# A state-space layer's entry and its scan: rows stored unscaled by column halves, scan cut into quarters

## The chip, the core and the metric

The kernel runs on one core of a Trainium2 chip. The metric is the device time of the whole program in microseconds (us). Engines are named as the profile names them: PE (matrix products; PEld are its weight loads), DVE (vector), ACT (activations and copies), POOL, and SP, whose queue (SPq) issues most DMAs. Each engine works through its own instructions in order; semaphores connect them.

## The reference, cut to what matters

The program is a two-layer encoder over 512 tokens of 1024 columns. The change touches the seam between the layers: the gated per-layer embedding that ends layer 0, the root-mean-square norm that opens layer 1, and the state-space mixer (S5) behind it.

```
h  = h + sigmoid(rmsnorm(h, norm_ple[0]) @ ple_gate[0]) * (p[0] @ ple_proj[0])
hn = rmsnorm(h, norm_mix[1])          # h * rsqrt(mean(h*h) + eps) * w
u  = hn.reshape(512 tokens, 64 groups, 16 columns)
# per group, 64 complex states, both directions of time:
#   state[t] = lam * state[t-1] + B u[t]      y[t] = Re(C state[t])
y  = s5(u) + backward s5(u) + d_skip * hn
out, gate = split(gelu(y) @ glu_w)    # glu_w: 1024 x 2048
h  = h + out * sigmoid(gate)
```

## The kernel before

A ring of six 1 MB tiles (`ring`, tile `n` in slot `n % 6`) holds every streamed matrix. SP loads tile `n` once tile `n - 6` is released (the list `release`); its queue is one ordered list, and other transfers stand at fixed places of it. ACT rounds each weight tile to a high part and DVE subtracts to get a low part (`split_tile`), after which PE multiplies (`split_product`, L1300). Product 1 is the embedding gate (two column halves of 512, groups `pg00` and `pg01`), product 2 the matrix `glu_w`.

**Entry.** ACT takes the sigmoid of each finished gate bank (L2131). When both halves of a token block `c` (128 tokens, four blocks) are there, DVE multiplies and adds (`embed_add`, L2819 and L2821, 1024 columns at a time). Then ACT squares, DVE scales rows by the norm factor and the weight (`norm(3)`, L2327), and SP moves the result (`s5_moves`): four stores to DRAM (L829), eight loads back (L834) with eight consecutive tokens per partition (`UN`, 64 chunks in each of two column halves, so 16 partitions per load), and the table of decays (L836). ACT waits for all nine loads, reorders by group into `UP` (L2141), PE transposes (L1601, 64 small ones), DVE copies to `U` (L2833).

**Chunk inputs.** PE forms, for each of 16 banks `b` of four groups, the contribution of each eight-token chunk to the states (`chunk_inputs`, L1615, products with only 64 moving columns). ACT drains each bank into `Z` (L2151).

**Scan.** `scan(dve, chain, hf)` runs on DVE for one half of the groups after the other (32 groups): seven steps of four instructions along the chunks of a block (128x512 each), six small ones across the eight blocks (128x64), seven more of four that spread the block starts (128x512). ACT copies each finished slice to `H` (`place_states`, two instructions of 64x512, L819 and L820); the backward direction is mirrored there.

**Outputs.** PE waits for all eight slices of a half (semaphore `s_zb`), then runs `outputs(q)` for four of the eight blocks `q` of eight groups (L1631 and L1634: per group one product with `U` and two with states, 24 per block), each in two banks; ACT applies gelu to each bank (L2161), PE transposes (`turn_outputs`, L1643), ACT and DVE write high and low parts (`gelu_high` L2167, L2840) for product 2. PE starts product 2 when all eight blocks are through.

Of the kernel before, what the change touches and what calls it, by code (L numbers as in the profile page):

```python
# [53 lines left out]
def build_program(nc, I, out):  # L54
# [27 lines left out]
    with ctx:  # L82
# [245 lines left out]
        s_hnd = sem("hn_in_dram")  # L328
        s_un = sem("s5_inputs_by_chunk")
        s_upA = sem("s5_inputs_by_group")  # L330
# [87 lines left out]
        def unit_after_block(i):  # L418
# [3 lines left out]
            if i == 3:  # L422
# [55 lines left out]

        f_high, f_low = [[sbuf_r[:, a:a + TILE].rearrange("p (k n) -> p k n", k=4)
                          for a in (ffa_end.at + m * TILE, ffa_end.at + (m + 1) * TILE)] for m in (0, 2)]  # L480
# [199 lines left out]
        HALF = G5 // 2  # L680
# [52 lines left out]
        def decays(ap):  # L733
# [3 lines left out]
        s5a = Arena(sbuf, base, words)  # L737
        U = s5a.take(G5 * NC5).rearrange("p (g n) -> p g n", g=G5)
        un_at = s5a.at
        UN = s5a.take(L5 * D // 2).rearrange("p (t n) -> p t n", t=L5)  # L740
        ZW = 2 * NC5 * HALF
        z_at = [s5a.at, s5a.at + ZW]
        h_at = [s5a.at + 2 * ZW, s5a.at]
        s5a.take(3 * ZW)
        Z, H = [[sbuf[:, a:a + ZW].rearrange("p (e s j g) -> p e s j g", e=2, s=8, j=8) for a in at] for at in (z_at, h_at)]
        lamR, lamI = decays(s5a.take(3 * L5 * G5))
        UP = sbuf[:, z_at[1]:z_at[1] + L5 * D // 2].rearrange("p (q g t c) -> p q g t c", q=4, g=8, t=L5)
        una = Arena(sbuf, un_at, un_at + L5 * D // 2)
        s_at = [una.at, una.at + 2 * 8 * HALF]
        S5 = [una.take(2 * 8 * HALF).rearrange("p (e s g) -> p e s g", e=2, s=8) for _ in range(2)]  # L750
        scan_tmp = [una.take(16 * HALF).rearrange("p (e s g) -> p e s g", e=2, s=8) for _ in range(2)]
        Yb = [una.take(L5 * P).rearrange("p (t n) -> p t n", t=L5) for _ in range(2)]
        gtmp = sbuf[:, base + 5 * D:base + 5 * D + 2048].rearrange(v4, a=4)
        hn_dram = nc.dram_tensor("hn_by_token", (T, D), F32, kind="Internal").ap()
# [4 lines left out]
            3: lambda e, c: e.wait_ge(s_ph, c + 1),  # L759
            4: lambda e, c: e.wait_ge(s_drD, cumD[gidx["go1"]] - 3 + c),  # L760
            5: lambda e, c: e.wait_ge(s_mc, c + 1),
            6: lambda e, c: e.wait_ge(s_ph, 4 + c + 1),
# [14 lines left out]
        def scan(dve, chain, hf):  # L777

            z, st, (a, b) = Z[hf], S5[hf], scan_tmp
            wide = [P, 2, 8, HALF]  # L780
            of_half = slice(HALF * hf, HALF * (hf + 1))
            real = lambda j: lamR[:, j - 1, of_half].unsqueeze(1).unsqueeze(1).broadcast_to(wide)
            imag = lambda j: lamI[:, j - 1, :, of_half].unsqueeze(2).broadcast_to(wide)

            def product_sum(old, swapped, j, add, new):
                chain.link(dve.tensor_tensor(new[0], old, real(j) if len(old.shape) == 4 else real(j)[:, :, 0, :], ALU.mult))
                chain.link(dve.tensor_tensor(new[1], swapped, imag(j) if len(old.shape) == 4 else imag(j)[:, :, 0, :], ALU.mult))
                dve.wait_ge(chain.sem, chain.n - 1)
                chain.link(dve.tensor_tensor(new[0], new[0], add, ALU.add))
                chain.settle()  # L790

            for j in range(1, 8):
                swapped = bass.AP(sbuf, z_at[hf] + ZW // 2 + (j - 1) * HALF, [[words, P], [-ZW // 2, 2], [8 * HALF, 8], [1, HALF]])
                product_sum(z[:, :, :, j - 1, :], swapped, 1, z[:, :, :, j, :], (a, b))
                chain.link(dve.tensor_tensor(z[:, :, :, j, :], a, b, ALU.add))
                chain.settle()
            chain.link(dve.memset(st[:, :, 0, :], 0.0))
            chain.link(dve.tensor_copy(st[:, :, 1, :], z[:, :, 0, 7, :]))
            chain.settle()
            for n in range(2, 8):  # L800
# [354 lines left out]
        def _(pe):  # L1155
# [490 lines left out]
            for q in range(8):  # L1646
                chunk_inputs(q)
# [1475 lines left out]
```

## Time and profile before

| | us |
|---|---|
| median of 3 runs (2834.9 to 2839.12) | 2835.84 |
| the profiled execution, as timed | 2841.83 |
| its span, first to last instruction | 2839.9 |
| its mean granted TensorE clock (1.00 is 2.4 GHz) | 0.938 |

PE is busy 89% of the span, DVE 60%, ACT 44%. All times of the trace count from the start of the span. The stretch of the change runs from 1122 us, where the gate product is under way, to 1334.7 us, where product 2 starts; everything behind depends on it. In the page's line of PE's busy tenths this stretch holds the lowest digits of the span's second half (4, 7, 6).

### The profile page before, as it was taken

The numbers are of one execution on the slowest core, as the hardware profiler recorded it, in microseconds if no ns is written. First come the engines' busy times: TensorE is split into PE (matmuls) and PEld (weight loads), VectorE is DVE, ScalarE is ACT, GpSimd is POOL, SyncE is SP. The second block draws the span as 40 slices with busy tenths as digits, with TensorE's granted clock in tenths as the row PEclk, the third lists the DMA queues.
The fourth block names the chain that finished last, engine by engine and source line by source line (L and its number), as shares of the span: only waits on it lengthen the run. The fifth ranks groups of instructions, "written<-read, shape, count | busy, mean of one in ns | idle before, by whom it ended". The sixth has DMA issues, their size and how long they took to land.

```text
span 2839.9 us, 31193 instructions
## 1 busy us (share of the span) xinstructions
PE 2539.9 (89%) x12509; PEld 2037.2 (72%) x12509; DVE 1700.9 (60%) x1870; ACT 1249.7 (44%) x1359; POOL 239.2 (8%) x240
## 2 busy tenths in 40 slices
PE   4889898889999998476949999999999999999977
PEld 2445464468887876476849988898889988898853
DVE  5697788332323223284256678766876778677852
ACT  2343333032222213353225567555765567566741
POOL 3012845000000000000000000000000000000010
PEclk9999989999999999558969999999999999999989
DMA  8446510122322231524046779877997689767950
GB/s 232 139 140 184 149 60 30 52 72 91 104 89 89 91 117 60 130 104 186 30 163 228 241 281 371 285 252 245 358 333 252 240 311 366 270 238 251 381 202 30
DMA packets 317023, 528.70 MB, mean 186 GB/s; under 512 B 19302, under 2 KB 175562, under 8 KB 314218
## 3 DMA queue, kind: packets, MB, share of 16 engines
q1 hardware_dynamic: 287690, 481.83, 49.6%
q0 software_dynamic: 6000, 26.27, 2.9%
q10 hardware_dynamic: 23184, 18.55, 2.0%
q8 instruction: 101, 1.65, 0.2%
q14 instruction: 48, 0.39, 0.0%
HBM read 497.05 MB, written 47.91 MB: 192 GB/s over the span
## 4 chain that ended last, share of the span: by engine, by line
PE 79%; DVE 9%; ACT 3%; issue 3%; POOL 3%; DMA 2%; SPq 0%; ACTq 0%; DVEq 0%; POOLq 0%
PE psum L1698 25%; PE psum L1300 16%; PE psum L1757 11%; PE psum L1558 5%; PE psum L1759 4%; PE psum L1198 4%; PE psum L1221 3%; PE psum L1615 2%; DVE stages_r L2994 1%; PE psum L1634 1%; ACT stages_r L2213 1%; PE psum L1369 1%; POOL stages L1023 1%; POOL stages L1026 1%; PE psum L1175 1%
## 5 line engine op out<-in xcount | busy, mean ns | idle before, releaser
L2994 DVE TENSOR_TENSOR stages_r<-kept,stages_r 128x2048 fp32r<-128x2048 f32 x336 | 769.1, 2291 | 274.0 <-ACT stages_r L2213 273.2
L1698 PE MATMUL psum<-stages_r 128*128 128x512 f32 x3136 | 751.7, 398 | 21.0 <-DVE stages_r L3049 11.1
L2213 ACT ACTIVATE stages_r<-kept 128x2048 fp32r<-128x2048 f32 x336 | 637.3, 1912 | 266.1 <-PE psum L1698 140.4
L1698 PEld LDWEIGHTS psum<-stages_r 128*128 128x128 f32 x3136 | 593.2, 191 | 149.5 <-DVE stages_r L2994 12.4
L1757 PE MATMUL psum<-stages_r 128*128 128x320 f32 x1792 | 464.8, 345 | 6.3 <-issue 3.2
L1300 PE MATMUL psum<-stages_r 128*128 128x512 f32 x1920 | 442.8, 393 | 17.2 <-DVE stages_r L2773 17.2
L1300 PEld LDWEIGHTS psum<-stages_r 128*128 128x128 f32 x1920 | 365.1, 190 | 94.2 <-issue 17.7
L1759 PE MATMUL psum<-stages_r 128*128 128x160 f32 x1792 | 423.1, 236 | 0.0
L1759 PEld LDWEIGHTS psum<-stages_r 128*128 128x128 f32 x1792 | 342.8, 191 | 2.0
L1757 PEld LDWEIGHTS psum<-stages_r 128*128 128x128 f32 x1792 | 337.0, 188 | 9.0 <-DVE stages_r L2994 3.8
L2773 DVE TENSOR_TENSOR stages_r<-kept,stages_r 128x2048 fp32r<-128x2048 f32 x54 | 123.5, 2292 | 363.1 <-ACT stages_r L2093 363.1
L2093 ACT ACTIVATE stages_r<-kept 128x2048 fp32r<-128x2048 f32 x54 | 103.1, 1915 | 349.8 <-PE psum L1300 245.9
L1558 PE MATMUL psum<-stages_r,stages_front_r 128*128 128x512 f32 x672 | 154.5, 392 | 6.8 <-DVE stages_front_r L2792 6.8
L1558 PEld LDWEIGHTS psum<-stages_r,stages_front_r 128*128 128x128 f32 x672 | 127.4, 190 | 33.8 <-issue 7.2
L1221 PE MATMUL psum<-stages,kept 128*128 128x512 f32 x256 | 118.5, 608 | 0.8 <-ACT stages L1860 0.8
L1198 PE MATMUL psum<-kept,stages 128*128 128x512 f32 x256 | 112.2, 600 | 1.6 <-ACT stages L1860 0.8
L2249 ACT ACTIVATE stages<-stages 128x160 f32<-128x160 f32 x112 | 37.8, 338 | 158.2 <-DVE stages L3026 158.2
L1198 PEld LDWEIGHTS psum<-kept,stages 128*128 128x128 f32 x256 | 49.1, 193 | 62.8 <-issue 60.8
L1105 POOL DMA_INDIRECT stages<-moe_rows_by_token,stages x8 | 18.3, 2290 | 891.6 <-PE psum L1706 521.4
L1221 PEld LDWEIGHTS psum<-stages,kept 128*128 128x128 f32 x256 | 47.2, 193 | 54.4 <-issue 53.3
L3029 DVE TENSOR_TENSOR kept<-stages 128x160 f32<-128x160 f32 x112 | 36.6, 327 | 45.2 <-ACT stages L2249 45.2
L1175 PE MATMUL psum<-kept,stages 128*128 128x128 f32 x160 | 26.7, 341 | 39.5 <-DVE stages L2327 39.2
(379 smaller groups left out, 2512.4 us busy)
## 6 DMA issues: line engine op xcount, KB each, us to landing
kept<-in_moe_w_gu_dram SPq DMA_DIRECT2D x224, 1024.0 KB, 6.5
kept<-in_moe_w_down_dram SPq DMA_DIRECT2D x112, 1024.0 KB, 6.4
kept<-in_ffn_w_gu_dram SPq DMA_DIRECT2D x28, 1024.0 KB, 5.1
kept<-in_ev_w_in_dram SPq DMA_DIRECT2D x16, 1024.0 KB, 6.4
kept<-in_ffn_w_down_dram SPq DMA_DIRECT2D x14, 1024.0 KB, 5.1
s_output_maps_by_state<-stages ACTq DMA_DIRECT2D x64, 128.0 KB, 2.0
s_input_maps<-stages ACTq DMA_DIRECT2D x32, 256.0 KB, 2.5
s_output_maps<-s_output_maps_by_state SPq DMA_DIRECT2D x32, 256.0 KB, 4.9
```

Source lines behind the costliest of these rows:

```text
L1198: m = pe.matmul(psum[:, b0 + b, 0:width], act[:, 4 * kk + k, b * P:(b + 1) * P], w[:, k, 0:width], **at)
L1221: m = pe.matmul(psum[:, b, :], *pair, start=kk == 0 and k == 0, stop=kk == 1 and k == 3)
L1300: m = pe.matmul(psum[:, 4 * (g % 2) + b, :], *pair, start=kk == 0 and k == 0 and n == 0, stop=kk == 1 and k == 3 and n == 2, skip_group_ch ...
L1558: m = pe.matmul(psum[:, 2 * c + hf, :], a[:, k, at], w[hf][:, k, :], start=j == 0 and k == 0 and n == 0, stop=j == FJ - 1 and k == 3 and n ...
L1615: m = pe.matmul(psum[:, b % 8, (2 * gl + e) * NC5:(2 * gl + e + 1) * NC5], w[:, 4 * i + gl, e, :], U[:, 8 * q + 4 * i + gl, :], start=True ...
L1698: m = pe.matmul(out_, a, b, start=start and n == 0, stop=stop and n == len(pairs) - 1, skip_group_check=True)
L1757: pe.matmul(bank[:, 0:2 * CAP], wh[:, k, fs], x_[:, k, :], start=k == 0, stop=False, skip_group_check=True)
L1759: m = pe.matmul(bank[:, 0:CAP], wl[:, k, fs], x_[:, k, 0:CAP], start=False, stop=k == 7, skip_group_check=True)
L2093: act.activation(f_high[t % 2], ring[:, n % RING, :].rearrange("p (k n) -> p k n", k=4), ACT.Copy).then_inc(s_wh, 1)
L2213: act.activation(w_high[n % WSLOTS], unit_tile(n), ACT.Copy).then_inc(s_wh, 1)
L2773: dve.tensor_tensor(f_low[t % 2], ring[:, (SPLIT_RUNS[run][1] + t) % RING, :].rearrange("p (k n) -> p k n", k=4), f_high[t % 2], ALU.subtr ...
L2994: dve.tensor_tensor(w_low[n % WSLOTS], unit_tile(n), w_high[n % WSLOTS], ALU.subtract).then_inc(s_ws, 1)
```

## The change

**Entry by halves.** The embedding is added for columns 0 to 511 as soon as gate group `pg00` is drained, and for the rest after `pg01` (`embed_half`). SP stores the half `h` unscaled and loads it back at once (`s5_rows(sp, j)`: four stores of 128x512, four loads of 16 partitions with 16 KB each); the first half stands in SP's queue ahead of two weight tiles, the second behind them. Sums of squares go by halves on ACT (`entry_squares`), are brought into the order of `UN` by eight small products on PE with a selection matrix `pick`, and give a factor `ers` per token. ACT and DVE apply it while they reorder into `UP` (four slices each); the norm weight comes in when DVE moves the transposes to `U` (`ew`). `norm(3)`, its weight load and the full-width add are gone, and the decays come last. PE transposes the first half of the groups, does two chunk blocks, then transposes the second.

**Scan by quarters.** `Z`, the states and the tables are cut into four quarters `v` of 16 groups. A move (`along`, `across`, `spread`) is four instructions; `advance` issues several independent moves together, so that one fills the other's waits. Spreading is by block `q` of eight groups, in two pieces `r` of four and three slices. `place_states(act, q, r)` follows each piece with 3 or 5 copies on ACT, standing between the gelus of the block before. PE waits for `s_zb >= q + 1` before each `outputs(q)`. The two wide waits before product 2 become waits for four parts each.

On SP's queue, first before. `s_input_maps` are 1 MB tiles for the chunk inputs; `dense_bank_done` ends a gate group.

```order
L897 DMA kept<-s_input_maps 128x2048 [waits dense_bank_done]
L897 DMA kept<-s_input_maps 128x2048 [waits ring_tile_used]
L897 DMA kept<-s_input_maps 128x2048 [waits dense_bank_done]
L829 DMA hn_by_token<-stages 128x1024 [waits hn_ready] x4
L834 DMA stages<-hn_by_token 16x8x512 [waits hn_in_dram]
```

And with the change:

```order
L951 DMA kept<-s_input_maps 128x2048 [waits dense_bank_done]
L878 DMA h_by_token<-kept 128x512 [waits ple_added] x4
L882 DMA stages<-h_by_token 16x4096 [waits h_in_dram] x4
L951 DMA kept<-s_input_maps 128x2048 [waits ring_tile_used]
L951 DMA kept<-s_input_maps 128x2048 [waits dense_bank_done]
L878 DMA h_by_token<-kept 128x512 [waits ple_added] x4
L882 DMA stages<-h_by_token 16x4096 [waits h_in_dram] x4
L887 DMA stages<-s_decays 128x1536 [waits dense_bank_done]
```

One half of the round trip has moved ahead of two tiles; the second stands behind them.

On ACT, before, at the start of the outputs. `s5_states_scanned` counts DVE's slices, `s5_y_done` PE's output banks.

```order
L819 ACTIVATE stages<-stages 64x16x32 [waits s5_states_scanned]
L820 ACTIVATE stages<-stages 64x2x8x32
L2161 ACT_TABLE_LOAD
L2161 ACTIVATE stages<-psum 64x4x8x16 [waits s5_y_done] x4
L2167 ACTIVATE stages_r<-psum 128x8x64 [waits gelu_transposed]
```

And with the change, from the second gelu of a block on:

```order
L2249 ACTIVATE stages<-psum 64x4x8x16 [waits s5_y_done]
L855 ACTIVATE stages<-stages 64x16x3x8 [waits s5_states_scanned]
L859 ACTIVATE stages<-stages 64x8x3x8 x2
L863 ACTIVATE stages<-stages 64x16x8
L864 ACTIVATE stages<-stages 64x2x8x8
L2255 ACTIVATE stages_r<-psum 128x8x64 [waits gelu_transposed]
L2249 ACTIVATE stages<-psum 64x4x8x16 [waits gelu_transposed,s5_y_done]
```

The placing of the next block has moved between the gelus; the five copies end what `outputs(q + 1)` waits for.

On DVE with the change, one call of `advance` in the second quarter: an `along` move (256 elements) beside both pieces of a `spread` (512 and 384).

```order
L837 TENSOR_TENSOR stages<-stages 128x256 [waits dve_chain]
L838 TENSOR_TENSOR stages<-stages 128x256
L837 TENSOR_TENSOR stages<-stages 128x512
L838 TENSOR_TENSOR stages<-stages 128x512
L837 TENSOR_TENSOR stages<-stages 128x384
L838 TENSOR_TENSOR stages<-stages 128x384
L842 TENSOR_TENSOR stages<-stages 128x256 [waits dve_chain]
L842 TENSOR_TENSOR stages<-stages 128x512 [waits dve_chain]
L842 TENSOR_TENSOR stages<-stages 128x384 [waits dve_chain]
```

Before, every second instruction of a step waited for the one just ahead of it.

```diff
@@ scan
-            for j in range(1, 8):
-                swapped = bass.AP(sbuf, z_at[hf] + ZW // 2 + (j - 1) * HALF, [[words, P], [-ZW // 2, 2], [8 * HALF, 8], [1, HALF]])
-                product_sum(z[:, :, :, j - 1, :], swapped, 1, z[:, :, :, j, :], (a, b))
-                chain.link(dve.tensor_tensor(z[:, :, :, j, :], a, b, ALU.add))
-                chain.settle()
...
+        SPREAD = ((4, 4), (1, 3))
+        def spread(q, r):
+            v, in_v, (j, n) = q // 2, slice(GB * (q % 2), GB * (q % 2 + 1)), SPREAD[r]
...
+        def advance(dve, chain, finals, done, *moves):
+            for kind, old, swapped, real, imag, add, new, (a, b) in moves:
+                if kind in done:
+                    dve.wait_ge(*done[kind])
+                chain.link(dve.tensor_tensor(a, old, real, ALU.mult))
+                chain.link(dve.tensor_tensor(b, swapped, imag, ALU.mult))
...
+        def place_states(act, q, r):
+            v, g0, (j, n) = q // 2, GB * (q % 2), SPREAD[r]
+            act.wait_ge(s_zf, 2 * q + r + 1)
+            at = slice(g0, g0 + GB)
+            act.activation(H[v].rearrange("p e s j g -> p (e s) j g")[0:NS, :, j:j + n, at], Z16[v][0:NS, :, j:j + n, at], ACT.Copy)
+            for e in range(2):
...
+                m = act.activation(backward, Z[v][NS:P, e, :, j:j + n, at], ACT.Copy)
+            if r:
...
+                act.activation(H[v][0:NS, :, :, 0, at], S5[v][0:NS, :, :, at], ACT.Copy)
+                m = act.activation(backward, S5[v][NS:P, :, :, at], ACT.Copy)
+                m.then_inc(s_zb, 1)
@@ SP
+        def s5_rows(sp, hf):
...
+                sp.dma_start(h_dram[hf, c * P:(c + 1) * P, :], half_h).then_inc(s_hnd, 16)
+            for c in range(TC):
+                sp.wait_ge(s_hnd, 16 * TC * (hf + 1))
...
+                if n == s5_tile0 + RING - 2:
+                    s5_rows(sp, 0)
                 if n == s5_tile0 + RING:
-                    s5_moves(sp)
+                    s5_rows(sp, 1)
+                    s5_decays(sp)
@@ PE
+            turn_inputs(0)
+            chunk_inputs(0)
+            chunk_inputs(1)
+            turn_inputs(1)
+            for q in range(2, 8):
+                chunk_inputs(q)
+            pe.wait_ge(s_vd, 16)
             for q in range(8):
-                chunk_inputs(q)
-            for q in range(8):
-                if q % 4 == 0:
-                    pe.wait_ge(s_vd, 16)
-                    pe.wait_ge(s_zb, 8 * (q // 4 + 1))
                 outputs(q)
-                if q % 4:
+                if q:
                     turn_outputs(q - 1)
...
-            pe.wait_ge(s_glA, 8)
-            pe.wait_ge(s_glD, 8)
+            turn_outputs(7)
             split_product(2)
@@ ACT
+            for t in range(L5 // 2):
+                act.activation(UP[:, :, :, t, :].rearrange("p q g c -> p (q g) c"), UN[:, t, :].rearrange("p (g c) -> p g c", c=GC),
+                               ACT.Copy, scale=ers[:, t:t + 1]).then_inc(s_entA, 1)
...
+            for r in range(2):
+                place_states(act, 0, r)
             for q in range(8):
-                if q % 4 == 0:
-                    place_states(act, q // 4)
-                gelu(2 * q)
-                gelu(2 * q + 1)
...
+                for r in range(2):
+                    gelu(2 * q + r)
+                    if q < 7:
+                        place_states(act, q + 1, r)
+                if q:
                     gelu_high(q - 1)
@@ DVE
+            for j in range(1, 8):
+                move(along(3, j), *([across(2, j)] if j > 1 else []), *(block(2 + j // 3) if j in (2, 5) else []))
+            turn_states(2)
+            first_super(3)
+            for n in range(2, 8):
+                move(across(3, n), *(block(3 + n // 2) if n in (2, 4) else []))
+            gelu_low(0)
+            gelu_low(1)
+            turn_states(3)
+            move(*block(6))
+            move(*block(7))
```

## Rows read from the trace of the kernel before

**Rows 1.** Busy time by windows (start:end, us, busy and count per engine, then PEclk, DMA)
```profile
1142.00:1178.00 36.00, 0.10 (x1) 0.00 (x0) 8.04 (x8) 6.98 (x12) 1.07 (x2) 0.55 0.87 197
1186.00:1200.00 14.00, 13.75 (x65) 13.75 (x65) 0.19 (x1) 6.22 (x6) 0.00 (x0) 0.50 0.20 76
...
1261.00:1265.00 4.00, 4.00 (x20) 4.00 (x21) 3.93 (x7) 1.07 (x1) 0.00 (x0) 0.50 0.00 0
1265.00:1287.00 22.00, 21.96 (x202) 21.32 (x201) 21.06 (x52) 7.28 (x11) 0.00 (x0) 1.00 0.38 145
...
1335.00:1340.00 5.00, 5.00 (x13) 3.84 (x13) 1.77 (x1) 0.00 (x0) 0.00 (x0) 0.50 1.03 382
```
**Rows 2.** The chain that ended last, 1153 to 1424 us (start, us, what)
```profile
1153.64 2.92 DMA hn_by_token<-stages
...
1161.71 15.61 DMA stages<-s_decays
...
1178.55 6.93 PE psum L1601 x64
...
1186.25 54.89 PE psum L1615 x256
...
1243.27 17.60 issue
...
1287.43 15.60 issue
...
1334.71 89.90 PE psum L1300 x384
```
**Rows 3.** The entry in order of time (start, us, engine, line, [idle before <-releaser])
```profile
1122.81 2.29 DVE L2773 TENSOR_TENSOR stages_r<-kept,stages_r 128x2048 fp32r<-128x2048 f32 x1 [9.01 <-ACT stages_r L2093]
...
1142.14 0.60 ACT L2131 ACTIVATE stages<-psum 128x512 f32<-128x512 f32 x1 [2.12 <-PE psum L1300]
...
1177.35 3.90 ACT L2141 ACTIVATE stages<-stages 128x1024 f32<-128x1024 f32 x4 [28.85 <-DMA stages<-s_decays]
```
**Rows 4.** Landing times: the eight loads of line 834, and the weight tiles
```profile
DMA to landing us min/median/max: 5.4/10.1/14.5
...
kept<-s_input_maps SPq DMA_DIRECT2D x8, 1024.0 KB, 4.8
```
**Rows 5.** The scan in order of time on DVE
```profile
1216.06 0.69 DVE L786 TENSOR_TENSOR stages<-stages 128x512 f32<-128x512 f32 x1 [29.86 <-ACT stages L2151]
1216.66 0.68 DVE L787 TENSOR_TENSOR stages<-stages 128x512 f32<-128x512 f32 x1
...
1218.71 0.69 DVE L786 TENSOR_TENSOR stages<-stages 128x512 f32<-128x512 f32 x1
...
1234.88 0.23 DVE L786 TENSOR_TENSOR stages<-stages 128x64 f32<-128x64 f32 x1
...
1235.67 0.22 DVE L786 TENSOR_TENSOR stages<-stages 128x64 f32<-128x64 f32 x1
```
**Rows 6.** ACT in order of time: the last drain, one placing copy, one gelu
```profile
1241.16 2.10 ACT L2151 ACTIVATE stages<-psum 64x512 f32<-64x512 f32 x2 [1.29 <-PE psum L1615]
1243.29 0.63 ACT L819 ACTIVATE stages<-stages 64x512 f32<-64x512 f32 x1
...
1268.48 0.59 ACT L2161 ACTIVATE stages<-psum 64x512 f32<-64x512 f32 x1 [2.08 <-PE psum L1634]
```
**Rows 7.** The page's groups by line: the smallest ACT copy (128x160, 338 ns)
```profile
L2249 ACT ACTIVATE stages<-stages 128x160 f32<-128x160 f32 x112 | 37.8, 338 | 158.2 <-DVE stages L3026 158.2
```
**Rows 8.** PE in order of time: a matmul after a gap; the transposes of one output block
```profile
97.66 1.03 PE L1256 MATMUL psum<-kept,stages 128*128 128x128 f32 x4 [2.82 <-ACT stages L1913]
...
1315.29 0.71 PE L1643 MATMUL psum<-kept,stages 64*128 64x64 f32 x8
```
**Rows 9.** Windows around two gaps of PE (columns as in Rows 1)
```profile
98.00:99.00 1.00, 1.00 (x5) 0.82 (x4) 0.00 (x0) 0.28 (x1) 1.00 (x1) 0.50 1.04 403
...
1082.90:1085.10 2.20, 0.00 (x0) 0.01 (x1) 2.17 (x4) 0.00 (x0) 0.00 (x0) 1.00 0.46 127
```

More of the change, by code:

```diff
@@ L679, in build_program @@
         M5 = L5 + 1
-        HALF = G5 // 2
+        QUARTERS = 4
+        QW = G5 // QUARTERS
+        GB = 8
         STEP = 2
@@ new lines, in build_program @@
+        pick = ent.take(pick_w)
+        pick_n = bass.AP(sbuf, ent.at - pick_w + NC5 - 16, [[words, P], [NC5, 2], [1, 16]])
+        pick_t = ent.take(L5)
+        ew_rows = ent.take(P).rearrange("p (t c) -> p t c", t=L5)
+        ew = ent.take(G5)
+        esc = ent.take(2 * TC * L5).rearrange("p (j c t) -> p j c t", j=2, c=TC)
+        erms, ers = [ent.take(L5) for _ in range(2)]
+        esq_junk = [ffa_end_junk[:, 512 * n:512 * (n + 1)] for n in range(2)]
+        ENT_SQUARE = lambda n: n + 1
@@ new lines, in advance @@
+        def advance(dve, chain, finals, done, *moves):
[4 more added lines that the diff above has]
+                chain.link(dve.tensor_tensor(b, swapped, imag, ALU.mult))
+            n = chain.n - 2 * len(moves)
+            for i, (kind, old, swapped, real, imag, add, new, (a, b)) in enumerate(moves):
+                dve.wait_ge(chain.sem, n + 2 * i + 1)
+                chain.link(dve.tensor_tensor(a, a, add, ALU.add))
+            n += 2 * len(moves)
+            for i, (kind, old, swapped, real, imag, add, new, (a, b)) in enumerate(moves):
+                dve.wait_ge(chain.sem, n + i + 1)
+                last = finals if kind[0] == "spread" else chain
+                last.link(dve.tensor_tensor(new, a, b, ALU.add))
+                done[kind] = (last.sem, last.n)
@@ L2825, in _ @@
             norm(2, parts=True)
-            for t in range(4):
-                split_tile(1, t)
-            embed_add(0)
-            norm(3, False)
+            split_tile(1, 0)
+            split_tile(1, 1)
+            by_chunk = ident.rearrange("p (n t) -> p n t", t=L5)
+            chain.link(dve.memset(pick, 0.0))
+            chain.link(dve.tensor_reduce(out=pick_t, in_=ident.rearrange("p (n t) -> p t n", t=L5), axis=AX_X, op=ALU.add))
+            chain.settle()
+            for i in range(2):
+                chain.link(dve.tensor_reduce(out=pick_n[:, i, :], in_=by_chunk, axis=AX_X, op=ALU.add))
@@ new lines, in move, with block @@
+            def move(*moves):
+                advance(dve, chain, finals, done, *moves)
+            def block(q):
+                return [spread(q, 0), spread(q, 1)]
+            inputs_in(0)
+            for j in range(1, 8):
+                move(along(0, j))
+            first_super(0)
+            for n in range(2, 8):
+                move(across(0, n))
+            turn_states(0)
+            inputs_in(1)
+            for j in range(1, 8):
+                move(along(1, j), *(block(j // 3) if j in (2, 5) else []))
@@ new lines, in _ @@
+            first_super(1)
+            inputs_in(2)
+            for j in range(1, 8):
+                move(along(2, j), *([across(1, j)] if j > 1 else []))
+            turn_states(1)
+            first_super(2)
+            inputs_in(3)
+            for j in range(1, 8):
+                move(along(3, j), *([across(2, j)] if j > 1 else []), *(block(2 + j // 3) if j in (2, 5) else []))
+            turn_states(2)
+            first_super(3)
+            for n in range(2, 8):
+                move(across(3, n), *(block(3 + n // 2) if n in (2, 4) else []))
```

320 lines of the change are left out of this document (198 added, 122 removed).

## The prediction

> **What bounds the kernel now.** I read the chain of waits first, then the windows of busy time, then each engine in order of time. The stretch between the two products is a chain of four parts with nothing beside it. The round trip through DRAM: the last gate sigmoid ends at 1142.7 [rows 3], the last store lands at 1156.6, the decays at 1177.3 behind all the loads [rows 2], and PE has worked 0.10 us of 36 [rows 1]. Transposes and chunk inputs: 1178.55 to 1241.2, PE never free [rows 2]. The scan: after ACT's last drain (1243.3) PE stands 17.6 us, and 15.6 us more between the two halves of the outputs [rows 2]. The outputs and the start of product 2, at 1334.71. What the change is worth is by how much it moves that last time, since product 2 and all behind it keep their length.
>
> **Entry.** DVE finishes its last weight tile at 1125.1 [rows 3] and then adds the first column half: eight instructions of 128x512. Their price I take from the scan. A step of four such instructions takes 2.65 us, one with 64 elements 0.79 [rows 5]; so 1.04 ns per element and 0.52 us of overhead per dependent step of four. Two dependent pairs make 2.9 us, four pairs 5.8, ending at 1130.9. The last store lands 2.9 us later [rows 2], 1133.8. Four loads follow, issued 0.6 us apart. Eight loads landed 5.4 to 14.5 us after their issue [rows 4], so one more every 0.64 + 9.1/7 = 1.94 us. The new loads have the same 256 KB and the same 16 partitions each; I keep the price. First half down at 1133.8 + 5.4 + 3 x 1.94 = 1145.0.
>
> SP has issued two weight tiles behind these loads, the second at about 1142.5. A 1 MB tile alone lands in 4.8 us [rows 4]. The decays landed last of the queue in the old order (15.6 us after issue, where a larger tile takes 4.8), so I take it that one queue is served in order: the tiles, some 2.6 us of transfer each, are through at about 1150, the four second stores (1 MB) about 1153. Without that queueing the stores would land 2.9 us after the add of the last block (1144.2), at 1147.1. Four loads: 1153.1 + 11.2 = 1164.3. ACT and DVE then build `UP` side by side: four ACT copies 3.9 us [rows 3], four on DVE of 1024 elements 4 x 1.14 = 4.6. PE begins at 1168.9 instead of 1178.55: **9.6 us gained**. Its ends: 19 (no queueing, and loads at the rate of tiles) and -7 (loads of 16 KB per partition at half the rate: 2 x 7.8 us more). Sums of squares, `pick`, the eight small products and the factors take no time: they need the last add at 1144.2 and have 20 us of DMA to hide under; without that cover, one square (0.6), a small add, a root and a reciprocal, under 3 us. The four added scalings on DVE are in the 4.6; the weight multiply replaces a copy of equal size. SP's third item, the decays, is wanted only when the scan starts, 17 us on.
>
> Chunk inputs take as long as before, 6.93 + 54.89 us; the second half of the transposes has only changed places. They run at half clock in both [rows 1]. ACT's last drain ends at 1233.7.
>
> **Scan.** `along` on 256 elements: 4 x 0.27 + 0.52 = 1.59 us a step. Beside another move the waits close: 0.60 us from one 512 to the next [rows 5] is 0.53 of elements and 0.07 of overhead, so `along` costs 1.35, `across` (32 elements) 0.41, a block of two spreads 4.3. First quarter: its four banks are drained at 1188.3 (3.5 of transposes, 13.7 of products, 2.1 of drain [rows 6] behind 1168.9); states known at 1204. Second quarter with blocks 0 and 1: from 1205.4 to 1225. Third with the second's `across`: 1238. Fourth with blocks 2 and 3: these end near 1245.5 and 1255; block 4 at 1264.3, block 5 at 1269.7, then two low parts, 6 at 1278.7, 7 at 1283.1.
>
> **Outputs.** After the drain ACT places block 0. A copy costs 0.63 us for 512 elements and 0.338 for 160 [rows 6, 7], so 0.83 ns per element and 0.205 fixed. First piece (512, 256, 256): 1.5; second (384, 192, 192, 128, 128): 1.9. PE starts at 1237.1. It starts at half clock as it did before: 4 us at 1.2 GHz held 20 matmul records, the 22 us behind at 2.4 GHz 202 [rows 1]. At full clock a bank takes 0.59 + 2.08 = 2.67 us from gelu to gelu [rows 6], so a block of two banks and 48 records 5.34, 9 records a us. With 4.1 us at 5 a us first, block 0 takes 7.2, each later one 5.34. Then comes the new wait. The last bank's gelu (0.59 [rows 6]) and the five copies of the second piece (1.9) stand between the end of block q and the start of q + 1: with two handovers of 0.1, 2.7 us, of which PE fills 0.71 with transposes [rows 8]. Behind those copies on ACT only `gelu_high` is queued, which has the next half block to run in. Pace 8.04 us per block. Outputs end at 1237.1 + 7.2 + 7 x 8.04 = 1300.6; the last gelu and eight transposes add 1.5: product 2 may start at 1302.1, **32.6 us earlier**. The entry's 9.6 is in it; so 23 comes from the scan. DVE is ahead of this pace throughout: block 4 is wanted at 1268.5 and is there at 1264.3, the least slack, 4 us.
>
> Product 2 began at half clock, after a gap, and held it for 5.3 us [rows 1, 2]. Now PE comes out of its transposes into it: +2.6 us. Its first tile is fetched when block 5 is out (1284.6) and split on ACT and DVE (2 and 2.3 us) from 1296.4: ready at 1300.7, in time by 1.4 us.
>
> **The clock in the gaps.** PE stands 1.9 us between blocks (2.6 before the second). The clock stayed at 2.4 GHz over an idle 2.2 us and had fallen to 1.2 after one of 2.82 [rows 8, 9]. So I count one fall: 4.1 us at half clock cost 2.0. From both sides: no fall, or one in each of seven gaps, 14.
>
> The Trainium skill ("TensorE: Matmul & The Clock Gate", A second HAM failure mode: psum-queue depth-cycling) says that short pauses between groups of matmuls which cycle through PSUM banks are enough to make the clock swing. By that rule the sum would be that of the first rival below; the row of the 2.2 us gap speaks against it, that of the 2.82 us gap for it.
>
> **The sum.** 32.6 + 2.6 - 2.0 = 33.2. The profiled execution took 2841.83 us (span 2839.9), 6.0 above the median; 2841.8 - 33.2 = 2808.6, and from the median of the runs shown 2835.84 - 33.2 = **2802.6 us**.
>
> **Rivals.**
> 1. *The clock falls in every gap.* For it: the 2.82 us row, and gaps of nearly that size. Against: the 2.2 us row; PE is dense for 5.3 us of 8. Seven falls instead of one: 12 more, 2815.
> 2. *DVE becomes the bound.* The spreads read and write runs of eight elements. ACT's strided drain costs 1.05 us where a copy of the same size costs 0.63 [rows 6], factor 1.67; on the 30 us of spread elements, 20 us more. Block 4 would come 12 us later against 4 of slack, block 7 20 against 9.5: 10 to the end, 2813. The Trainium skill ("Vector Engine (DVE) Microarchitecture Reference", Measured stream behaviour on trn2) says that DVE keeps its full rate as long as elements come in adjacent pairs or longer runs, and loses it only on single hops. By it this rival is void; the drain's single hops and the price of 1.67 agree with it in kind, though they are ACT's.
> 3. *The loads do not keep their rate.* One descriptor per partition instead of eight. At half rate the first loads also delay tiles and stores: 16 worse, 2819. Against: eight loads went by at one steady rate.
> 4. *Slower than before.* The clock stays at half through all outputs, as it stays there for the whole of the chunk inputs though PE is busy 13.75 of 14 us [rows 1]. The place is the gap between blocks; it decides from the point where PE stands there longer than it takes the clock to fall and never climbs. That needs copies of short runs at the drain's price: second piece 3.1 us, placing block 0 5.6, gap 3.9, blocks 10.2 at half clock. 1233.7 + 5.7 + 10.2 + 7 x 14.1 + 2.9 = 1351, 16.5 later than before and the same cold start: 2852. Against: twice the same matmuls lifted the clock after 4 us.
>
> That the change doesn't do what it says isn't open in the order: the halves and quarters stand where the diff puts them. But PE still waits for all 16 drains before the first output, so scan and outputs overlap with each other and not with the chunk inputs; the sum has that.
>
> **How the numbers follow.** The forecast 73%, rival 1 12%, rival 2 6%, rival 3 5%, rival 4 3%, something else 1%. The forecast's own range is 2791 to 2811: 10 down for an entry without queueing and no falls, 8 up for a queue served worse or two or three falls. To leave out no more than 2 in 10 the range reaches over rivals 1 and 2: 2790 to 2818. About 0.2%, 5.7 us, is what a measurement can tell. All cases but rival 4 lie below that: faster 0.95; same 0.02, where two rivals meet; slower 0.03.
>
> **What would show it.** The `UP` slices start near 1164 and the first transposes at 1169; stores of the second half that land 9 us after their add, not 3 (if 3, I am 6 too high). ACT's last drain at 1234. The first output block 7.2 us, later ones 5.3 with 2.7 between starts; a granted clock of 1.00 in nearly all of them. DVE's last spread near 1283, before the last block is wanted. Product 2 at 1302, at full clock. It is wrong if DVE, not ACT's copies, ends the wait of the output blocks, if the clock is 0.50 in them, or if loads take more than 2 us each.

## The result, and the profile after

| | before | after |
|---|---|---|
| median of four runs each, us | 2837.48 (2834.9 to 2839.84) | 2808.14 (2805.14 to 2811.3) |
| ratio, 95% interval | | 0.9897 [0.988, 0.9914] |
| profiled execution: time, span | 2841.83, 2839.9 | 2807.0, 2805.0 |
| mean granted clock of TensorE | 0.938 | 0.944 |
| gate sigmoid (start) to product 2 (start) | 192.6 | 162.2 |
| product 2, us | 89.90 | 87.27 |

The forecast was 2802.6 us; the median is 5.5 above it. The profiled execution is 34.8 us shorter than that of before, where the sum said 33.2.

The chain that ended last, after, over the stretch of [rows 2]:
```profile
1141.60 0.60 ACT stages L2198
...
1143.67 7.49 DMA h_by_token<-kept
...
1152.47 9.08 DMA stages<-h_by_token
1161.64 2.57 ACT stages L2229 x4
1164.45 3.65 PE psum L1671 x32
1168.10 13.84 PE psum L1685 x64
1181.94 3.60 PE psum L1671 x32
1185.54 41.16 PE psum L1685 x192
...
1228.83 3.27 issue
1232.10 0.66 PE psum L1702 x2
```
The chain has the same parts, but the decays no longer end the round trip, the last load of the second half does. PE starts at 1164.45 instead of 1178.55. The two waits of 17.6 and 15.6 us [rows 2] are gone: ACT's placing of the first block holds PE for 3.27, and between the blocks PE now waits seven times, once 2.49 us and six times 1.85, 13.6 in all.

ACT, DVE and SP in order of time at the end of the entry:
```profile
1161.64 2.56 ACT L2229 ACTIVATE stages<-stages 128x512 f32<-128x512 f32 x4 [13.64 <-DMA stages<-h_by_token]
```
```profile
1161.65 1.67 DVE L2956 TENSOR_SCALAR stages<-stages 128x512 f32<-128x512 f32 x4 [13.42 <-DMA stages<-h_by_token]
```
```profile
L882 SPq DMA_DIRECT2D stages<-h_by_token x8: 318/418/420, 1131.9 to 1152.5; - x8
...
DMA to landing us min/median/max: 4.2/7.0/9.3
```
The `UP` slices have 512 elements per partition, not the 1024 of [rows 3], since both halves now lie side by side over 128 partitions.

PE in order of time, four of the eight starts of an output block, and the transposes ahead of one:
```profile
1242.53 0.43 PE L1702 MATMUL psum<-kept,stages 128*64 128x128 f32 x2 [2.49 <-ACT stages L864]
1247.93 0.71 PE L1714 MATMUL psum<-kept,stages 64*128 64x64 f32 x8
1250.49 0.43 PE L1702 MATMUL psum<-kept,stages 128*64 128x128 f32 x2 [1.85 <-ACT stages L864]
...
1260.11 0.43 PE L1702 MATMUL psum<-kept,stages 128*64 128x128 f32 x2 [1.85 <-ACT stages L864]
...
1269.73 0.43 PE L1702 MATMUL psum<-kept,stages 128*64 128x128 f32 x2 [1.85 <-ACT stages L864]
```
Every wait ends with ACT's last placing copy (line 864), none with DVE. ACT in the gap before the second of them:
```profile
1248.04 0.59 ACT L2249 ACTIVATE stages<-psum 64x512 f32<-64x512 f32 x1 [0.66 <-PE psum L1705]
1248.66 0.52 ACT L855 ACTIVATE stages<-stages 64x384 f32<-64x384 f32 x1
1249.19 0.61 ACT L859 ACTIVATE stages<-stages 64x192 f32<-64x192 f32 x2
1249.81 0.31 ACT L863 ACTIVATE stages<-stages 64x128 f32<-64x128 f32 x1
1250.13 0.31 ACT L864 ACTIVATE stages<-stages 64x128 f32<-64x128 f32 x1
```
One gelu and five copies, 2.4 us, priced at 2.5. Windows over the outputs and the start of product 2 (columns of [rows 1]):
```profile
1242.50:1248.00 5.50, 5.47 (x49) 5.35 (x50) 5.50 (x23) 1.94 (x4) 0.00 (x0) 1.00 0.00 1
1248.00:1250.50 2.50, 0.65 (x10) 0.51 (x9) 2.50 (x7) 2.38 (x7) 0.00 (x0) 1.00 0.53 157
1250.50:1254.00 3.50, 3.50 (x18) 3.50 (x19) 3.50 (x14) 1.09 (x1) 0.00 (x0) 0.56 0.99 414
...
1261.00:1265.00 4.00, 4.00 (x24) 4.00 (x23) 3.93 (x14) 0.65 (x2) 0.00 (x0) 0.57 0.01 4
...
1269.70:1277.70 8.00, 6.12 (x57) 5.86 (x57) 7.97 (x17) 5.44 (x12) 0.00 (x0) 1.00 0.83 349
...
1303.80:1309.00 5.20, 5.20 (x24) 4.31 (x24) 4.30 (x3) 3.23 (x3) 1.44 (x2) 1.00 0.99 357
```
Here the reader is to see 49 matmuls in 5.5 us at 1.00, behind the gap of 2.49 us, and 18 in 3.5 us at 0.56, behind a gap of 1.85. Behind another gap of 1.85 us (at 1269.70) the clock kept 1.00. Where it fell, the next block starts 9.6 us later instead of 8.0. It fell behind four of the seven gaps. Product 2 runs at full clock from its start.

DVE in order of time, spreads of the first quarter and the last instruction of the last spread:
```profile
1204.25 0.68 DVE L837 TENSOR_TENSOR stages<-stages 128x512 f32<-128x512 f32 x1
1204.85 0.69 DVE L838 TENSOR_TENSOR stages<-stages 128x512 f32<-128x512 f32 x1
1205.45 0.55 DVE L837 TENSOR_TENSOR stages<-stages 128x384 f32<-128x384 f32 x1
...
1278.07 1.15 DVE L847 TENSOR_TENSOR stages<-stages 128x512 f32<-128x512 f32 x2
```
A spread of 512 elements in runs of eight takes 0.68 us, as the plain runs did [rows 5].

### The profile page after: what moved, and what is told of

It reads as the page before. It is cut to its first block, busy times and chain, and to the rows that moved or that the text cites. A ratio compares the mean times of both kernels' runs of the same rounds, so it can differ in the third digit from the quotient of the medians.

```text
span 2805.0 us, 31451 instructions
## 1 busy us (share of the span) xinstructions
PE 2545.2 (91%) x12526; PEld 2041.9 (73%) x12526; DVE 1708.8 (61%) x2010; ACT 1254.3 (45%) x1400; POOL 240.2 (9%) x240
## 3 DMA queue, kind: packets, MB, share of 16 engines
q8 instruction: 102, 1.67, 0.2%
## 4 chain that ended last, share of the span: by engine, by line
PE 80%; DVE 9%; ACT 4%; POOL 3%; issue 2%; DMA 2%; ACTq 0%; POOLq 0%; DVEq 0%; SPq 0%
PE psum L1768 25%; PE psum L1356 16%; PE psum L1827 11%; PE psum L1614 6%; PE psum L1829 4%; PE psum L1251 4%; PE psum L1274 3%; PE psum L1685 2%; DVE stages_r L3181 1%; PE psum L1705 1%; ACT stages_r L2303 1%; PE psum L1425 1%; POOL stages L1077 1%; POOL stages L1080 1%; PE psum L1332 1%
## 5 line engine op out<-in xcount | busy, mean ns | idle before, releaser
L1274 PE MATMUL psum<-stages,kept 128*128 128x512 f32 x256 | 119.2, 611 | 0.8 <-ACT stages L1930 0.8
L1425 PE MATMUL psum<-stages,kept 128*128 128x512 f32 x128 | 60.5, 607 | 0.0
```

The costliest lines, as they stand in the source:

```text
L1274: m = pe.matmul(psum[:, b, :], *pair, start=kk == 0 and k == 0, stop=kk == 1 and k == 3)
L1425: m = pe.matmul(bank, w[:, k, b * P:(b + 1) * P], hnT[:, n, :], **at)
```

## The experiments

Each kernel is the changed one with the edit shown. The profiled executions arrive at the entry between 1141.0 and 1147.1 us (the start of the second group of small products of line 1657, those of the second column half), and no edit touches what that point waits for. So the table gives, beside the median, the time from there to the start of product 2 in the profiled execution, which is free of that spread. The ratio is to the kernel before, run beside each (its median was 2837.48 us beside the first result, 2838.68 beside the next four runs, 2839.28 beside the four behind them, 2839.07 beside the last).

| | median us | ratio | line 1657 to product 2 |
|---|---|---|---|
| after (first result) | 2808.14 | 0.9897 [0.988, 0.9914] | 158.0 |
| unchanged, again | 2806.57 | 0.9885 [0.9869, 0.9902] | 160.3 |
| gaps filled | 2803.98 | 0.9873 [0.9857, 0.989] | 151.7 |
| placed sooner | 2797.75 | 0.9854 [0.9837, 0.987] | 146.7 |
| rows ahead | 2802.41 | 0.9869 [0.9853, 0.9886] | 153.9 |
| halves together | 2818.22 | 0.9928 [0.9912, 0.9944] | 168.2 |
| four blocks | 2825.72 | 0.9953 [0.9938, 0.9969] | 175.3 |
| moves in turn | 2806.42 | 0.9884 [0.9868, 0.99] | 158.0 |
| sooner and ahead | 2791.02 | 0.983 [0.9816, 0.9844] | 142.4 |
| blocks sooner | 2788.44 | 0.9821 [0.9808, 0.9835] | 144.2 |

**Unchanged, again.**

> The changed kernel itself, again, beside the runs it is to be compared with. If its first four times (2805.1 to 2811.3, median 2808.1) are typical, it comes to 2805 to 2811 again. The scatter of 6 us is what falls of TensorE's clock between output blocks could make: four falls in the profiled execution, at 1.7 us each; with none to seven falls the time would move by up to 12.

2806.57 us (2805.51 to 2808.05), 32.1 under the kernel before beside it. The clock fell behind five of the seven gaps here (1.65 us more), the entry was 1.1 us longer, and the first block took 0.5 less: that is the 2.3 us between the first two rows of the table. The same kernel thus spreads by 2.3 us in this stretch.

**Does the clock in the gaps cost what the windows say?** PE fills the gap with matmuls on data at hand, whose results nobody reads (the added wait keeps them out of a bank that DVE still reads):
```diff
                     turn_outputs(q - 1)
+                if q < 7:
+                    if q >= 4:
+                        pe.wait_ge(s_glD, q - 3)
+                    for _ in range(7 if q else 10):
+                        pe.matmul(psum[0:NC5, q % 4, 0:P], U[:, 0, :], ident, start=True, stop=True)
```


> PE fills each gap between two output blocks with matmuls whose result nobody reads (7 of 64 weights by 128 columns behind the transposes, 10 in the first gap, where no transposes stand). Theory: in the gaps the clock falls to 1.2 GHz, and four blocks of the profiled execution were 1.7 us longer for it. With the gaps filled the clock stays at 1.00 from block 1 on, all blocks come 8.0 us apart, product 2 starts near 1297 instead of 1303.8, and the time is 6 to 7 us below the changed kernel. Rival: the filling delays the next block or the placing copies set the pace anyway; then the clock is 1.00 and the time the same or up to 2 us more.

A window over the outputs, and one block's start:
```profile
1243.00:1297.00 54.00, 52.61 (x473) 49.72 (x471) 42.69 (x119) 35.58 (x71) 0.00 (x0) 1.00 0.46 176
```
```profile
1267.72 0.43 PE L1702 MATMUL psum<-kept,stages 128*64 128x128 f32 x2 [0.18 <-ACT stages L864]
```
The clock stays at 1.00 and all blocks are 7.96 to 7.99 us apart. From line 1657 to product 2 that is 6.3 us less than in the first profile, for four falls of 1.65, and 8.6 less than in the second. The median fell by 2.6 only, where 6 to 7 were expected. The two profiled executions differ by 2.8: this one arrived 3.9 us later at the entry, was 8.6 shorter to product 2, and 1.9 longer behind it; neither the late arrival nor the 1.9 was traced. The price of the falls is shown by the profile; the medians alone would not carry it.

**What sets the gap?** ACT places both pieces of block q + 1 ahead of the second gelu of block q:
```diff
-                for r in range(2):
-                    gelu(2 * q + r)
-                    if q < 7:
-                        place_states(act, q + 1, r)
+                gelu(2 * q)
+                for r in range(2 if q < 7 else 0):
+                    place_states(act, q + 1, r)
+                gelu(2 * q + 1)
```


> ACT places both pieces of block q + 1 between the two gelus of block q, so no copies stand between the end of a block and the next. Theory: the new wait of the outputs is ACT's queue (gelu 0.59 and copies 1.8), not DVE. Then PE waits 0.4 us behind its transposes instead of 1.9, the clock does not fall, blocks come 6.4 us apart until DVE becomes the bound at blocks 4 to 6 (its spreads end at 1261, 1266, 1275, 1279 and placing adds 3.1); product 2 starts near 1292, 12 us earlier, 2796. Rival: DVE is already the bound behind ACT's waits; then the gap stays near 2 us and the gain is under 3 us.

PE in order of time:
```profile
1248.69 0.43 PE L1702 MATMUL psum<-kept,stages 128*64 128x128 f32 x2 [0.59 <-ACT stages L864]
1255.40 0.43 PE L1702 MATMUL psum<-kept,stages 128*64 128x128 f32 x2 [0.60 <-ACT stages L864]
1264.46 0.43 PE L1702 MATMUL psum<-kept,stages 128*64 128x128 f32 x2 [2.94 <-ACT stages L864]
```
Gaps of 1.85 us become 0.6 (the first 1.17), behind which the clock never fell, and the pace is 6.7 us. 11.3 us less from line 1657 to product 2; the median is 8.8 less. The one long wait is that of block 4, whose placing now waits 2.4 us for DVE's spread: the slack that the prediction had put there is used up. Behind that wait the clock fell.

**Is the second half held up in SP's queue?** Its stores and loads are issued ahead of the two late weight tiles:
```diff
                     s5_rows(sp, 0)
+                    s5_rows(sp, 1)
                 if n == s5_tile0 + RING:
-                    s5_rows(sp, 1)
```


> The stores and loads of the second column half stand ahead of the fifth and sixth weight tile in SP's queue instead of behind. Theory: one queue is served in order, and the stores landed 7.5 us after the last add because 1 MB of tile was ahead of them. Then they land 3 us after the add (1146.7 instead of 1151.2), the UP slices start at 1157 instead of 1161.6, and all behind comes 4.5 us earlier; the tiles come at 1160 to 1163, long before 1199. Rival: the landing time of a store is its own latency behind whatever else moves; then it stays at 7 us and the time does not change.

The chain:
```profile
1143.06 2.11 DMA h_by_token<-kept
...
1146.48 9.44 DMA stages<-h_by_token
```
The last store lands 2.1 us after the add instead of 7.5. PE stands 11.7 us before its transposes, not 16.8 (17.9 in the unchanged kernel's second profile). The tiles that come later delay nothing: from PE's first transposes to the first output it is 67.6 us in both kernels.

The order of issue has a second part in this. SP, before and with the edit:
```profile
1133.68 8.26 SPq L951 DMA_DIRECT2D kept<-s_input_maps  x2
1141.98 2.02 SPq L878 DMA_DIRECT2D h_by_token<-kept  x4
```
```profile
1134.90 8.48 SPq L878 DMA_DIRECT2D h_by_token<-kept  x4
```
In the changed kernel SP itself could not issue the second tile until 1141.6, so that three stores whose data were ready went out just ahead of the last one. With the edit they went out as their data came. How the 5.4 us divide between the tiles and these stores wasn't tried. The median fell by 4.2 us.

**What are the halves worth?** All eight stores behind both tiles, then all eight loads, each of which waits for all stores (the function's two loops now run over both halves):
```diff
-                if n == s5_tile0 + RING - 2:
-                    s5_rows(sp, 0)
                 if n == s5_tile0 + RING:
-                    s5_rows(sp, 1)
+                    s5_rows(sp, (0, 1))
```


> Edit against the changed kernel: the eight h stores (both column halves) are issued together behind both late tile loads, and the eight row loads together behind them, each load waiting for all eight stores; amount of traffic, sizes and arithmetic stay. Theory (the half-split is worth it because the first half's four loads, about 1.8 us each, are already done when the second half's stores land at 1151.2): the eight loads run one after another, about 1.75 us each with 2.9 us for the first, and end at 1151.5 + 16.5 = 1168 instead of 1160, so the first PE transposes come 7 us later (at 1171 to 1172 instead of 1164.5) and the time is 6 to 8 us above the changed kernel. Rival (only the last stores' landing decides, eight loads overlap in their fixed part): at most 2 us later. Rival on the other side (the first half's loads hold back the second half's stores in the queue): the stores land earlier, at about 1149, and the time is 0 to 2 us shorter.

The chain, and the landing of the loads:
```profile
1147.41 7.10 DMA h_by_token<-kept
...
1157.67 15.26 DMA stages<-h_by_token
```
```profile
DMA to landing us min/median/max: 4.5/10.1/15.3
```
10.2 us more to product 2 than in the first profile, against 7 expected (11.7 in the median against the unchanged kernel): the eight stores take 9.6 us behind the last add (four took 7.5) and the eight loads 18.4 (four took 10.4). The landing times are near those of [rows 4]: the layout per partition left the rate of the loads alone. The rival of overlapping loads falls.

**What is the handing over by single blocks worth?** PE waits for four blocks, and ACT places four ahead of each group (its loop isn't shown):
```diff
-                pe.wait_ge(s_zb, q + 1)
+                pe.wait_ge(s_zb, 4 * (q // 4) + 4)
```


> Edit against the changed kernel: output block q waits until the spreads of all four blocks of its group are done (counts 4 and 8 instead of q+1), and ScalarE places the states of four blocks ahead of the group; VectorE's order and all arithmetic stay. Theory (what the change gains in the scan is that outputs start behind one block's spread and run beside the scan of the rest): outputs 0 to 3 start behind block 3's spread and its placing, near 1253, then go without gaps at about 5.5 to 6 us each to 1277, outputs 4 to 7 start behind block 7's spread (1279) and four placings (about 4 us), near 1284, and end at 1307; with the last gelus and the split the product starts at 1312 to 1320 instead of 1303.8: 8 to 16 us above the changed kernel. Rival (the blocks' gaps of 1.9 us and the clock falls cost as much as the early start gives): within 2 us of the changed kernel.

PE in order of time:
```profile
1251.69 0.66 PE L1702 MATMUL psum<-kept,stages 128*64 128x128 f32 x2 [28.01 <-issue]
1290.50 0.69 PE L1702 MATMUL psum<-kept,stages 128*64 128x128 f32 x2 [13.90 <-ACT stages L864]
```
17.3 us more to product 2, and 19.2 in the median; 8 to 16 were expected. Two long waits are back. DVE's adds that end a move, the last of them at 1281.2, and from the chain the first and the last block that ACT places for the second group:
```profile
L847 DVE TENSOR_TENSOR stages<-stages x64: 180/425/685, 1190.6 to 1281.2; 128x256 f32<-128x256 f32 x24, 128x32 f32<-128x32 f32 x24, 128x512 f32<-128x512 f32 x8, 128x384 f32<-128x384 f32 x8
```
```profile
1277.76 0.63 ACT stages L855
...
1287.29 0.63 ACT stages L855
```
The second wait was ACT's, not DVE's: it placed four blocks one after the other, 12.7 us where the expectation had counted 4, though blocks 4 and 5 had been spread long before. With only block 7 left to place behind its spread (1281.8 and 3.2 us) the outputs could have begun at 1284.9 instead of 1290.5. So 5.6 of the 17.3 us, as an estimate, are this edit's own placing order, and the handing over by single blocks is worth about 12.

**Is the interleaving of two moves needed?** One after the other:
```diff
-                advance(dve, chain, finals, done, *moves)
+                for one in moves:
+                    advance(dve, chain, finals, done, one)
```


> Edit against the changed kernel: VectorE advances the two pieces that go side by side one after the other, so its dependent operations follow each other directly in place of alternating with the other piece's. Theory: each dependent pair costs about 0.1 us more than an interleaved one (0.45 against 0.34 us pace at 128x256), the scan from 1202 to the last spread gets 10 to 14 us longer, the last spread ends near 1291 instead of 1279, outputs of block 4 and of the last blocks wait for VectorE, and the time is 3 to 7 us above the changed kernel (5 us or more of the delay hidden behind the output blocks' 8 to 9.6 us pace). Rival (VectorE's lead over the output blocks, 6 to 10 us, hides it all): within 1 us of the changed kernel, with the last spread later all the same.

The end of DVE's last spread, in this kernel and in the unchanged one:
```profile
1281.41 0.56 DVE L847 TENSOR_TENSOR stages<-stages 128x384 f32<-128x384 f32 x1
```
```profile
1276.33 1.16 DVE L847 TENSOR_TENSOR stages<-stages 128x512 f32<-128x512 f32 x2
```
DVE ends 4.5 us later (5.4 counted from PE's first transposes) and not 10 to 14, and the time is the same (2806.42 against 2806.57): my theory fell, the rival holds. Of the four instructions of a 128x512 move only the last add starts later behind the one before (0.72 us where the others have 0.60), so running in turn loses little, and the lead over the output blocks hides it.

**The two improvements together**, placed sooner and rows ahead:

> Both improvements measured singly before, together: the second half's rows are stored ahead of the two late tile loads in SyncE's queue (alone 4.2 us under the changed kernel), and ScalarE places the states of block q+1 ahead of the second gelu of block q (alone 8.8 us under it). Theory (the two act in stages that follow each other, entry and outputs): they add, 12 to 13 us under the changed kernel, about 2794, ratio to the kernel before 0.984. Against adding (block 4's outputs waited 2.9 us for VectorE's spread, and an earlier entry moves VectorE's scan only if the scan starts behind it): the scan's start moves with the transposes, so that wait stays and nothing is lost. Rival: the tiles that now load later are needed by the next layer's start, and 2 to 4 us are given back there: about 2797, the same as the placing alone.

2791.02 us, 15.6 under the changed kernel (2806.57) where 12 to 13 were expected. They add: the stretch to product 2 is 15.6 us shorter than in the first profile, against 11.3 and 4.1 singly. PE waits for block 4:
```profile
1255.51 0.69 PE L1702 MATMUL psum<-kept,stages 128*64 128x128 f32 x2 [2.95 <-ACT stages L864]
```
**Can DVE's order take that wait away?** On top of the two edits:
```diff
             first_super(2)
-            inputs_in(3)
-            for j in range(1, 8):
-                move(along(3, j), *([across(2, j)] if j > 1 else []), *(block(2 + j // 3) if j in (2, 5) else []))
+            for n in range(2, 8):
+                move(across(2, n), *(block(1 + n // 2) if n in (2, 4) else []))
             turn_states(2)
+            inputs_in(3)
+            for j in range(1, 8):
+                move(along(3, j), *(block(4 + j // 3) if j in (2, 5) else []))
             first_super(3)
             for n in range(2, 8):
-                move(across(3, n), *(block(3 + n // 2) if n in (2, 4) else []))
+                move(across(3, n))
```


> x7_sooner_and_ahead with VectorE's order changed: quarter 2 is carried across ahead of quarter 3's march along time, with blocks 2 and 3 spread beside it, and blocks 4 and 5 are spread beside the march of quarter 3; quarter 3 is carried across by itself. The operations are the same. In the run before it VectorE was over 96% busy from 1190 to 1271 and the outputs of blocks 3 and 4 waited 1.4 and 2.9 us for a spread. Theory (in that version VectorE's order bounds blocks 3 and 4): block 4's spread ends about 10 us sooner, both waits shrink to 0.6 us, blocks 0 to 5 follow each other every 6.7 us; block 6 needs VectorE's spread at about 1266 to 1268 as before and may wait 1 us for it; product 2 starts 2 to 3 us sooner: about 2788.5. Rival (VectorE's total bounds the end: the waits move from blocks 3 and 4 to blocks 6 and 7): within 1 us of the version before, 2791.

PE in order of time, and a window to the end of the last spread:
```profile
1257.38 0.43 PE L1702 MATMUL psum<-kept,stages 128*64 128x128 f32 x2 [0.59 <-ACT stages L864]
...
1270.06 0.69 PE L1702 MATMUL psum<-kept,stages 128*64 128x128 f32 x2 [6.55 <-ACT stages L864]
```
```profile
1190.00:1271.50 81.50, 65.94 (x461) 64.29 (x461) 79.44 (x247) 53.31 (x92) 0.00 (x0) 0.75 0.47 176
```
The waits at blocks 3 and 4 went, and one of 6.6 us came at block 6. DVE is busy 79.4 of 81.5 us, and ahead of block 6's spread stand the carrying across of quarter 3 by itself (3.9 us) and two low parts (2.0). The wait moved, as the rival said. That DVE's total bounds the end is not shown: an order with the second low part behind that spread wasn't tried. The stretch to product 2 got no shorter (144.2 against 142.4), the median is 2.6 lower with overlapping ranges. It meets the 2788.5 of the theory, but not by its mechanism, since product 2 did not start sooner; whether the version is faster at all stays open. Both are the fastest here.

## Why the prediction was right

The sign, the mechanism and the size held. That the total is as close as it is, 30.4 us to product 2 against 30.6, is partly luck: the entry, from the start of the last gate sigmoid to PE's first transposes, gave 13.6 instead of 9.6, and the part from the last drain to product 2 gave 16.5 instead of 21.0 (23.0 less 2.0 for the clock). The two misses nearly cancelled.

- *Entry.* Forecast 1168.9 for PE's start, measured 1164.45: 14.1 us sooner instead of 9.6, of which 0.5 is an earlier arrival. Landing of the second stores was 1.9 us sooner (1151.2 against 1153.1), the four loads took 10.4 us and not 11.2, and `UP` 2.6 and not 4.6, since I had given its slices 1024 elements. After the first landing a load took 2.06 us, not 1.94, just over the 2 that the prediction had named as a sign of being wrong; the four were sooner all the same because the first landed after 4.2 us and not 5.4. Rival 3 is void: between 1151.2 and 1161.5 the trace counts 64 packets of over 8 KB, one of 16 KB for each partition of the four loads, and their rate is nearly that of the eight loads before. The queue, on which that term rested, is shown by the run with the rows ahead; of the 14.1 us, 10.2 hang on the halves. What the rest owes to the norm and the decays leaving the chain wasn't tried.
- *Two slips in the working* changed nothing: the lower end written as -7 is -6 by its own terms (9.6 - 15.6), and its price gives 2.65 for two dependent pairs, not 2.9; in the first half two pairs took 2.66.
- *Chunk inputs, placing.* Last drain 1228.83, first output 1232.1: 4.9 and 5.0 under the entries of the sum, which is the entry's 4.5 and 0.4 more; placing took 3.27 us against 3.4.
- *Scan on DVE.* Blocks 4 and 7 were spread by 1261.0 and 1279.2, forecast 1264.3 and 1283.1, which is most of the entry's gain again. No output waited for DVE. Rival 2 is void: the runs of eight keep the full rate. This is what the Trainium skill ("Vector Engine (DVE) Microarchitecture Reference", Measured stream behaviour on trn2) states for adjacent pairs and longer runs, and the trace agrees (0.68 us for 512).
- *Outputs.* A gap of 1.85 us and 0.7 of transposes, a pace of 7.97 at full clock: forecast 1.9, 0.7 and 8.04. The first block took 7.9 us, not 7.2. The worth of this overlap is the 17 us that come back when four blocks are handed over together, less the estimated 5.6 of that edit's own placing.
- *The clock.* This term was mis-sized. I counted one fall for 2.0 us; there were four at 1.65, 6.6 us. The step that failed read one row of an idle 2.2 us at 1.00 as a proof for gaps of that size. Rival 1 (a fall in each gap) would have been as wrong: the truth lay between. Rival 4 (the clock never climbs) did not come: it rose within the first block and behind every fall. The rule of the Trainium skill ("TensorE: Matmul & The Clock Gate", A second HAM failure mode: psum-queue depth-cycling) warns of such pauses; this trace agrees for four gaps of seven, and with the pauses at 0.6 us the swing was gone.
- *Product 2.* A warm start, 2.63 us against 2.6. It came at 1303.8, forecast 1302.1, and its first tile was ready 1.5 us ahead (forecast 1.4).

From gate sigmoid to product 2: 30.4 us less, forecast 30.6 (32.6 - 2.0). With 2.6 of the warm start that makes 33.0 of the profile's 34.8; 0.5 is an earlier arrival, the rest lies elsewhere and wasn't traced. The median came out 5.5 above the forecast. Of that, 1.6 is the reference: I took off from 2835.84, and with a fourth run the median of before is 2837.48. The other 3.9 is a smaller gain between the medians, 29.3 us instead of 33.2; in the repetition it was 32.1. The profiled pair shows 34.8 because the execution of before that was profiled was a long one, 4.4 us above the median of its kernel, and that of after 1.1 below.

## What to carry to other kernels

Where two engines hand work over in blocks, put the copies that the next block needs ahead of the work that only this block's end needs: here that order was worth more than half of the 15.6 us still to be had. Look at what is queued ahead of a small transfer on its own queue: issuing the rows before two weight tiles delayed nothing and gave 4.2 us. When an engine is over 95% busy in front of what others wait for, look at all that stands ahead of each result before reordering: here the reordering moved the wait from blocks 3 and 4 to block 6.

## What the runs showed of the hardware

- Behind idle gaps of TensorE of one and the same length (1.85 us, between blocks of some 5.4 us) the clock sometimes fell and sometimes not. In the first profile it kept, fell, fell, kept, fell, fell, kept, over seven gaps (the first 2.49 us long); the runs with the moves in turn and with the halves together had the same order, the unchanged one fell, kept, fell, fell, kept, fell, fell. With the rows ahead it fell, fell, kept, fell, kept, fell, fell, so there is no fixed pattern; what decides wasn't tried. Each fall cost 1.65 us. In all, it fell behind 22 of the 35 gaps of 1.85 to 2.49 us in these five profiles. Behind the 25 gaps of 0.18 to 1.39 us in the runs with the gaps filled, placed sooner, sooner and ahead, and blocks sooner it never did; behind their three waits of 2.94, 2.95 and 6.55 us the block each time ran at 0.50 at first or soon after its start.
- A store of 256 KB landed 2.1 us after the data were there with nothing unfinished ahead of it in its queue, and 7.5 with two 1 MB tiles and three stores ahead.
- The loads onto 16 partitions kept the DMA engines as busy as the tiles and stores did, at under a third of their rate (windows of the first profile with tiles and stores, then with loads, columns of [rows 1]). Why wasn't tried.
```profile
1143.00:1145.00 2.00, 0.00 (x0) 0.00 (x0) 0.78 (x2) 1.99 (x7) 0.00 (x0) 1.00 1.05 426
...
1155.00:1157.00 2.00, 0.00 (x0) 0.00 (x0) 0.00 (x0) 0.00 (x0) 0.00 (x0) 0.50 1.02 123
```
- The four scalings of 128x512 took 1.67 us on DVE and 2.56 on ACT.
